# A two-layer decoder trunk on one core: the expert weights of one token block written by accumulating transfers

## The chip, the core and the metric

The kernel runs on one core of a Trainium2 chip. The metric is the device time of one execution in microseconds, the median of several runs. Five engines work beside each other and meet at semaphores: TensorE (PE in the profile) multiplies matrices, VectorE (DVE) and ScalarE (ACT) work element by element, GpSimd (POOL) mostly issues DMAs here, the row fetches among them, and SyncE (SP) issues the loads of the weight panels. Sixteen DMA engines serve all queues together.

## The reference

Two layers, each of a mixer block (three causal token mixers, gated and projected) and an expert block, on 512 tokens of width 1024, all in float32. The change touches the expert block:

```python
def block(xt):                       # 128 tokens at a time
    q = (xt @ w_pq).reshape(PEER_BLOCK, PEER_HEADS, 2, PEER_HALF)
    s = jnp.einsum('thpd,hpkd->thpk', q, sub_keys)
    v1, i1 = lax.top_k(s[:, :, 0], PEER_TOPK)
    v2, i2 = lax.top_k(s[:, :, 1], PEER_TOPK)
...
    top, pos = lax.top_k(cand, PEER_TOPK)
    eidx = jnp.take_along_axis(cidx, pos, axis=-1)
    g = jax.nn.softmax(top.astype(jnp.float32), axis=-1).astype(xt.dtype)
    ue = u_tab[eidx]
    a = jax.nn.gelu(jnp.einsum('thkd,td->thk', ue, xt))
    ve = v_tab[eidx]
    return jnp.einsum('thk,thkd->td', g * a, ve)
```

There are 8 heads, 128 x 128 = 16384 experts a layer, and each token takes 16 experts of each head, 128 in all.

## The kernel before

**Tokens.** The four tiles of 128 tokens are treated in two ways. Tiles 0 to 2, 384 tokens (SD), go densely: every expert's activation is computed for every token, gelu(u_tab @ h), 128 panels of 128 experts a layer, and multiplied by a weight that is zero for nearly all. Tile 3 (DB) goes sparsely: GpSimd fetches the 128 chosen rows of each token from u_tab with indirect DMAs (gather_u, line 700, into six buffers urow), and DVE makes a dot of each (line 1656); later the rows of v_tab follow the same way (gather_v).

**A panel.** A weight panel of 1024 x 128 is loaded by SP into one of four raw buffers, rounded to its high part by ACT (split_hi, line 418), its low part made by DVE (split_lo, line 428), both LEAD = 2 panels ahead, and multiplied by TensorE in 24 matmuls (gemm, lines 441 to 443): 512 columns for the query panels, 384 for the dense experts. ACT takes the output of an expert panel through gelu into hst (post_u, line 1196) and spills it to h_d in device memory. Two PSUM banks alternate.

**Order of a layer's second part.** The heads' stage: for each of 8 heads two query panels and T_U = 8 expert panels, and beside them on DVE the choice of the 16 best (best, rest, pairs, pairs_at, pairs2, places, and key_of in the first two panels of the next head). Behind the last head come the exponential and the division of the softmax for all heads at once, the addresses idu of the row fetches, and 8 more expert panels (M_R1) beside which the first fetches and dots run. Then N_G = 48 groups (M_G): in each an expert panel, and for 8 tokens a one-hot matmul (line 981, each in two passes) that turns the chosen keys and weights of a token into its 128 x 128 weights. DVE builds the one-hot tiles (hot, lines 1665 and 1667), ACT scales one of them (line 1223) and copies the result into stage (line 1247); every fourth group GpSimd writes a block of TB = 32 tokens, 2 MB, to g_d in device memory (line 727). Then 8 more expert panels (M_R2) and the second half: 128 panels of v_tab, for which h_d and g_d are read back (load_h, load_g), multiplied by DVE (weight, line 1698), split and multiplied by TensorE (lines 1001 to 1003), with the sparse tile's v rows beside them (line 1015).

**Queues.** GpSimd's DMAs are one queue in program order, and its waits hold all that follows. It spills and reloads the mixer's gates, loads parameters, fetches rows, writes g_d and reads h_d and g_d. DOTS tells how many dots (and fetches six rows ahead of them) stand beside each panel.

**Start.** norm_h(0, 0) scales the eight chunks of x; DVE makes columns of the modulation in between (first_columns). The first two panels are multiplied pairwise (gemm_two, lines 457 to 459), chunk by chunk as they come, but only when both low splits are there; these stand in the chunk iterations 7 and 8.

## Time and profile before

| | before |
|---|---|
| median of 3 runs | 3568.3 us (3566.43 to 3577.35) |
| the profiled execution | 3572.08 us, its span 3570.3 us |
| TensorE busy | 97% of the span |
| VectorE, ScalarE, GpSimd busy | 69%, 41%, 25% |
| mean granted TensorE clock | 0.986 |
| DMA | 909.83 MB, mean 255 GB/s |

In the profile a row of the time order gives start and duration in us, then engine, line, operation, out<-in and count, and in brackets the idle time of the engine before it with what ended it. Matmuls overlap, so the time that one costs is read from start to start. Numbers of a stretch are busy times of each engine in it. Times count from the span's start.

### The profile page before, as it was taken

The page shows a single profiled execution, that of the slowest core. Times are in us where ns is not written, and L with a number is a line of the kernel's source. Part 1 is how long each engine was busy: PE and PEld are TensorE (multiplying, and loading weights), DVE is VectorE, ACT ScalarE, POOL GpSimd, SP SyncE. Part 2 cuts the span into 40 slices and gives each one's busy share as a digit, 9 for nine tenths or more (in the row PEclk, how much of TensorE's full clock was granted, in tenths as well). Part 3 has the DMA queues.
Part 4 walks back from the last instruction along what each step waited for, and adds up shares of the span by engine and source line. Part 5 has one row for each costly group of instructions (what it writes and reads, how often), then busy time and mean ns, then how long its engine had stood idle before and what let it go on. Part 6 is the DMA issues. An engine that isn't in the chain of part 4 may idle for free.

```text
span 3570.3 us, 54219 instructions
## 1 busy us (share of the span) xinstructions
PE 3475.4 (97%) x18428; PEld 2973.7 (83%) x18428; DVE 2467.0 (69%) x4643; ACT 1462.7 (41%) x2544; POOL 895.4 (25%) x1026
## 2 busy tenths in 40 slices
PE   6999999999999999999999999999999999999998
PEld 5776889999999787777777777999999998777776
DVE  6455678889888775555464556888898878555554
ACT  3324233335877333333233333333367753333332
POOL 0010100003333534444400010000053345344442
PEclk9999999999999999999999999999999999999999
DMA  6354434447999998999744433444499999799995
GB/s 244 126 185 135 142 132 147 149 149 282 354 338 346 391 343 336 363 358 359 292 151 155 161 130 123 149 154 147 147 349 345 344 361 388 278 366 356 364 356 199
DMA packets 269536, 909.83 MB, mean 255 GB/s; under 512 B 32213, under 2 KB 65029, under 8 KB 268453
## 3 DMA queue, kind: packets, MB, share of 16 engines
q0 software_dynamic: 126352, 471.34, 35.9%
q1 hardware_dynamic: 106128, 385.92, 30.8%
q10 hardware_dynamic: 36868, 50.35, 3.8%
q8 instruction: 84, 1.38, 0.2%
q14 instruction: 104, 0.84, 0.1%
HBM read 792.14 MB, written 115.34 MB: 254 GB/s over the span
## 4 chain that ended last, share of the span: by engine, by line
PE 92%; DMA 3%; DVE 2%; issue 1%; POOL 1%; ACT 1%; SPq 0%; DVEq 0%; ACTq 0%; POOLq 0%
PE ps L441 15%; PE ps L443 15%; PE ps L442 15%; PE ps L1001 10%; PE ps L1003 9%; PE ps L1002 9%; PE ps L981 5%; PE ps L1015 3%; PE ps L810 2%; DMA urow<-in_u_rows,idu 1%; PE ps L866 1%; PE ps L937 1%; PE ps L485 1%; DMA hin<-expert_spill 1%; PE ps L887 1%
## 5 line engine op out<-in xcount | busy, mean ns | idle before, releaser
L441 PE MATMUL ps<-mov,whl 128*128 128x384 f32 (+1 forms) x2816 | 1008.8, 358 | 2.2 <-DVE whl L428 2.2
L443 PE MATMUL ps<-mov,whl 128*128 128x384 f32 (+1 forms) x2816 | 985.5, 350 | 0.0
L442 PE MATMUL ps<-mov,whl 128*128 128x384 f32 (+1 forms) x2816 | 984.2, 350 | 0.0
L428 DVE TENSOR_TENSOR whl<-raw,whl 128x1024 fp32r<-128x1024 f32 x648 | 792.5, 1223 | 206.8 <-ACT whl L418 202.5
L418 ACT CAST whl<-raw 128x1024 fp32r<-128x1024 f32 x648 | 679.5, 1049 | 87.4 <-ACT hst L1196 78.8
L1001 PE MATMUL ps<-whl,wgthl 128*128 128x512 f32 x1536 | 608.4, 396 | 19.6 <-DVE wgthl L1710 19.6
L700 POOL DMA_INDIRECT urow<-in_u_rows,idu x256 | 310.8, 1214 | 1208.8 <-DVE idu L1643 778.1
L1003 PE MATMUL ps<-whl,wgthl 128*128 128x512 f32 x1536 | 604.6, 394 | 0.0
L1002 PE MATMUL ps<-whl,wgthl 128*128 128x512 f32 x1536 | 603.4, 393 | 0.0
L441 PEld LDWEIGHTS ps<-mov,whl 128*128 128x128 f32 x2816 | 529.3, 188 | 40.1 <-issue 8.7
L442 PEld LDWEIGHTS ps<-mov,whl 128*128 128x128 f32 x2816 | 529.5, 188 | 30.5 <-issue 2.4
L443 PEld LDWEIGHTS ps<-mov,whl 128*128 128x128 f32 x2816 | 528.5, 188 | 31.6
L1256 ACT CAST wgthl<-wgt 128x384 fp32r<-128x384 f32 x256 | 131.4, 513 | 813.9 <-PE ps L1003 743.8
L1710 DVE TENSOR_TENSOR wgthl<-wgt,wgthl 128x384 fp32r<-128x384 f32 x256 | 142.7, 558 | 358.1 <-ACT wgthl L1256 356.8
L1001 PEld LDWEIGHTS ps<-whl,wgthl 128*128 128x128 f32 x1536 | 290.2, 189 | 108.1 <-issue 25.2
L1003 PEld LDWEIGHTS ps<-whl,wgthl 128*128 128x128 f32 x1536 | 290.1, 189 | 64.3
L1002 PEld LDWEIGHTS ps<-whl,wgthl 128*128 128x128 f32 x1536 | 290.3, 189 | 63.2
L708 POOL DMA_INDIRECT vrow<-in_v_tab,idv x256 | 272.6, 1065 | 252.2 <-PE ps L1015 183.4
L1656 DVE CUSTOM_DVE_ANT_0 urow<-urow,htok 128x1024 f32<-128x1024 f32 x256 | 306.3, 1218 | 34.4 <-DMA urow<-in_u_rows,idu 34.1
L1196 ACT ACTIVATE hst<-ps 128x384 f32<-128x384 f32 x256 | 123.9, 484 | 364.3 <-PE ps L443 344.0
L1223 ACT ACTIVATE hotg<-hotg,gT 128x128 f32<-128x128 f32 x768 | 235.1, 391 | 11.2 <-DVE hotg L1665 11.2
L690 POOL DMA_DIRECT2D hin<-expert_spill x256 | 145.0, 571 | 336.2 <-DVE wgt L1698 315.6
(261 smaller groups left out, 3623.0 us busy)
## 6 DMA issues: line engine op xcount, KB each, us to landing
raw<-in_uT_tab SPq DMA_DIRECT2D x256, 512.0 KB, 4.5
raw<-in_v_tab SPq DMA_DIRECT2D x256, 512.0 KB, 6.9
expert_spill<-hst ACTq DMA_DIRECT2D x256, 192.0 KB
hin<-expert_spill POOLq DMA_DIRECT2D x256, 192.0 KB, 7.9
gt<-weight_spill POOLq DMA_DIRECT2D x64, 768.0 KB, 8.8
weight_spill<-stage POOLq DMA_DIRECT2D x22, 2048.0 KB, 14.7
raw<-in_w_in SPq DMA_DIRECT2D x72, 512.0 KB, 4.7
raw<-in_w_mod SPq DMA_DIRECT2D x64, 512.0 KB, 3.6
```

The lines of the kernel that those rows point to most:

```text
L418: nc.scalar.copy(whl[:, m % RING, 0], raw[:, raw_n(m) % RAW]).then_inc(hi_done, 1)
L428: nc.vector.tensor_tensor(whl[:, m % RING, 1], raw[:, raw_n(m) % RAW], whl[:, m % RING, 0].bitcast(F32), ALU.subtract).then_inc(lo_done, 1)
L441: nc.tensor.matmul(o, w[:, 0, k], src[:, 0, k, :cols], start=(k == 0), stop=False)
L442: nc.tensor.matmul(o, w[:, 0, k], src[:, 1, k, :cols], start=False, stop=False)
L443: mm = nc.tensor.matmul(o, w[:, 1, k], src[:, 0, k, :cols], start=False, stop=(k == KC - 1))
L700: pool.indirect_dma_start(urow[:, k % UR], None, u_rows, bass.IndirectOffsetOnAxis(idu[:, k:k + 1], 0)).then_inc(u_in[k % UR], 16)
L708: pool.indirect_dma_start(vrow[:, slot], None, v_tab.rearrange("a p d -> (a p) d"), bass.IndirectOffsetOnAxis(idv[:, q, j:j + 1], 0)).then ...
L1001: nc.tensor.matmul(o, ghi, hi, start=first, stop=False)
L1002: nc.tensor.matmul(o, ghi, lo, start=False, stop=False)
L1003: mm = nc.tensor.matmul(o, glo, hi, start=False, stop=last)
L1223: ins = nc.scalar.activation(one, one, ACT.Copy, scale=gT[:, e * GT + t:e * GT + t + 1])
L1656: nc.vector.tensor_tensor_reduce(urow[:, k % UR], urow[:, k % UR], htok[:], 1.0, 0.0, ALU.mult, ALU.add, act_in[:, k:k + 1]).then_inc(dot_ ...
```

## The change

One of the three dense tiles, tokens 256 to 383 (N_TS = 1, OHB = 2), gets its weights in another way. Its four blocks of g_d are filled with zeros at the start of each layer's mixer, four DMAs of 2 MB in GpSimd's queue from a zero tile. In the heads' stage DVE computes, one head later, the place in g_d of each of the tile's 16 choices (chosen, seven small operations), and GpSimd adds the weight there with one indirect accumulating DMA for each choice, 128 elements of 4 bytes, one for each token: 16 a head, 128 a layer. For that the softmax is made head by head: the subtraction in places, the exponential on ACT at panel 9, the division on DVE at panel 10 (shares). Before a head's transfers GpSimd waits until the previous head's have landed; the last head's are put one by one among the row fetches behind the stage, and the reading of g_d waits for all.

The groups fall from 48 to 32 a layer, T_U grows from 8 to 10, so the number of panels stays. Of the sparse tile's 128 dots, 28 a layer go into the heads' stage, four for each head from the second on, at panels 9, 10, 11 and 11, with their fetches; DOTS_V is 21 instead of 24. The transposes that feed the fetches' dots (htok) move to the start of the heads' stage, and eight instead of eleven transposes turn the choices. At the very start the high splits of the first two panels stand in chunk iterations 1 and 3, the low ones in 3 and 5.

```diff
-T_U = 8
+T_U = 10
...
-LATE_U = 2 * REST + NTB * BLK_U
-DOTS_V = 24
+LATE_U = 2 * REST + N_G
+DOTS_H = (0, 0, 0, 0, 0, 0, 0, 0, 0, 1, 1, 2)
+DOTS_A = sum(DOTS_H) * (PH - 1)
+DOTS_V = 21
...
+            for b in range(N_OH, NTB):
+                pool.dma_start(g_d[:, :, b].rearrange("a p x -> p a x"),
+                               zero[:].unsqueeze(1).to_broadcast([P, P // AG, P])).then_inc(zero_out, 16)
...
+            def scatter_one(h, n):
+
+                k, t = h * TOPK + n // N_TS, n % N_TS
+                settle(pool)
+                pool.indirect_dma_start(g_d.rearrange("a p b (x o) -> (a p b x) o", o=1),
+                                        bass.IndirectOffsetOnAxis(idg[:, t, k:k + 1], 0),
+                                        topv[:, OHB + t].rearrange("p h k -> p (h k)")[:, k:k + 1], None,
+                                        compute_op=ALU.add).then_inc(sc_out, 16)
+
+            def scatter(h):
+
+                pool.wait_ge(idg_ready, l * PH + h + 1)
+                pool.wait_ge(g_norm, l * PH + h + 1)
+                pool.wait_ge(sc_out, l * (16 * N_TS * SLOTS) + 16 * N_TS * TOPK * h)
+                for n in range(N_TS * TOPK if h + 1 < PH else 0):
+                    scatter_one(h, n)
+
+            pool.wait_ge(zero_out, (l + 1) * (16 * (NTB - N_OH)))
+            for h in range(PH):
+                pool.wait_ge(idu_ready, l * PH + h + 1)
+                if h == 0:
+                    for k in range(UR):
+                        gather_u(k)
+                scatter(h)
+                if h + 1 < PH:
+                    for k in range(h * sum(DOTS_H), (h + 1) * sum(DOTS_H)):
+                        gather_u(k + UR)
+            left = list(range(N_TS * TOPK))
             for n in range(LATE_U):
-                for k in range(dots_by(n - 1) if n else 0, dots_by(n)):
+                for k in range(dots_by(n - 1) if n else DOTS_A, dots_by(n)):
                     if k + UR < SLOTS:
                         gather_u(k + UR)
+                    if left:
+                        scatter_one(PH - 1, left.pop(0))
...
-                if not (l or which) and c >= KC - 3 and c < KC - 1:
-                    split_hi(act, l, c - (KC - 3))
+                if not (l or which) and c in (1, 3):
+                    split_hi(act, l, c // 2)
...
+                    if j == 9:
+                        act.wait_ge(g_sub, l * PH + h + 1)
+                        nc.scalar.activation(topv[:, :, h], topv[:, :, h], ACT.Exp).then_inc(g_exp, 1)
...
-                if not (l or which) and c >= KC - 1:
-                    split_lo(dve, l, c - (KC - 1))
+                if not (l or which) and c in (3, 5):
+                    split_lo(dve, l, c // 2 - 1)
...
+            def chosen(h):
+
+                hs = slice(h * TOPK, (h + 1) * TOPK)
+                first, second = sel1[:, OHB:DB, h], sel2[:, OHB:DB, h]
+                nc.vector.scalar_tensor_tensor(idf[:, 0, hs], sel1[:, DB, h], float(NKEYS), sel2[:, DB, h], ALU.mult, ALU.add)
+                nc.vector.scalar_tensor_tensor(place[:, 1], second, float(NTB * AG), first, ALU.mult, ALU.add)
+                chain.link(nc.vector.tensor_scalar(place[:, 0], first, -1.5, 0.25, ALU.add, ALU.mult))
+                nc.vector.tensor_scalar(idu[:, hs], idf[:, 0, hs], lbase[:], None, ALU.add).then_inc(idu_ready, 1)
+                chain.link(nc.vector.tensor_scalar(place[:, 0], place[:, 0], MAGIC, MAGIC, ALU.add, ALU.subtract))
...
             for h in range(PH):
                 for j in range(2 + T_U):
                     split_lo(dve, l, M_T + h * (2 + T_U) + j + LEAD)
                     if j < 2 and h:
                         key_of(h - 1, j)
+                    if j == 1 and h:
+                        chosen(h - 1)
+                    if j == 10:
+                        shares(h)
+                    if h:
+                        at = (h - 1) * sum(DOTS_H)
+                        dots_between(at + sum(DOTS_H[:j]), at + sum(DOTS_H[:j + 1]))
```

## Rows read from the trace of the kernel before

**Rows 1.** The page: busy us, share, instructions; the chain by engine.

```profile
PE 3475.4 (97%) x18428; PEld 2973.7 (83%) x18428; DVE 2467.0 (69%) x4643; ACT 1462.7 (41%) x2544; POOL 895.4 (25%) x1026
...
PE 92%; DMA 3%; DVE 2%; issue 1%; POOL 1%; ACT 1%; SPq 0%; DVEq 0%; ACTq 0%; POOLq 0%
```

**Rows 2.** Stretches of layer 0: busy us, granted clock, DMA share, GB/s.

```profile
462.00:828.00 366.00, 366.00 (x2046) 351.06 (x2044) 310.87 (x954) 126.32 (x164) 0.00 (x0) 1.00 0.45 148
...
862.00:1146.00 284.00, 283.70 (x1903) 283.41 (x1902) 252.09 (x295) 224.20 (x527) 105.52 (x85) 1.00 0.98 346
```

**Rows 3.** TensorE in time order, two groups of one-hot matmuls.

```profile
903.31 1.95 PE L981 MATMUL ps<-hotg,hot 128*128 128x128 f32 x16
905.01 0.42 PE L441 MATMUL ps<-mov,whl 128*128 128x384 f32 x1
...
909.26 0.94 PE L981 MATMUL ps<-hotg,hot 128*128 128x128 f32 x7
```

**Rows 4.** ScalarE in time order, heads' stage: two panels' output copies.

```profile
533.97 0.49 ACT L1196 ACTIVATE hst<-ps 128x384 f32<-128x384 f32 x1 [2.11 <-PE ps L443]
...
538.13 0.49 ACT L1196 ACTIVATE hst<-ps 128x384 f32<-128x384 f32 x1 [2.11 <-PE ps L443]
```

**Rows 5.** All engines in time order, the end of the first normalization.

```profile
36.71 0.72 ACT L1084 ACTIVATE mov<-ht,mod_cols 128x512 fp32r<-128x512 f32 x1 [3.49 <-DVE ht L1346]
...
43.48 0.75 DVE L1351 SCALAR_TENSOR_TENSOR mov<-ht,mod_cols,mov 128x512 fp32r<-128x512 f32 x1
...
48.83 1.22 DVE L428 TENSOR_TENSOR whl<-raw,whl 128x1024 fp32r<-128x1024 f32 x1
...
50.20 0.79 PE L457 MATMUL ps<-mov,whl 128*128 128x512 f32 x1 [19.18 <-DVE whl L428]
```

**Rows 6.** Stretches again: start-up, and the mixer's first panels.

```profile
35.00:40.00 5.00, 0.00 (x0) 0.00 (x0) 4.89 (x11) 1.44 (x2) 0.00 (x0) 1.00 0.25 98
65.00:105.00 40.00, 40.00 (x169) 30.70 (x168) 24.97 (x26) 16.10 (x23) 0.00 (x0) 1.00 0.59 202
```

**Rows 7.** Instructions grouped by line: busy us, mean ns, idle before them.

```profile
L700 POOL DMA_INDIRECT urow<-in_u_rows,idu x256 | 310.8, 1214 | 1208.8 <-DVE idu L1643 778.1 <-DVE act_in L1656 393.6 <-issue 36.5
L1656 DVE CUSTOM_DVE_ANT_0 urow<-urow,htok 128x1024 f32<-128x1024 f32 x256 | 306.3, 1218 | 34.4 <-DMA urow<-in_u_rows,idu 34.1
```

**Rows 8.** VectorE in time order, heads' stage and first rest panels.

```profile
520.65 0.89 DVE L1544 MAX8 v<-ps 128x8 f32<-128x128 f32 x4 [2.28 <-PE ps L937]
...
548.50 0.23 DVE L1600 CAST abf<-abu 128x128 f32<-128x128 uint32 x1
...
552.68 1.23 DVE L428 TENSOR_TENSOR whl<-raw,whl 128x1024 fp32r<-128x1024 f32 x1 [2.69 <-ACT whl L418]
...
843.39 1.22 DVE L1656 CUSTOM_DVE_ANT_0 urow<-urow,htok 128x1024 f32<-128x1024 f32 x1 [2.32 <-DMA urow<-in_u_rows,idu]
```

**Rows 9.** ScalarE in time order, behind the last head.

```profile
827.69 1.28 ACT L1214 ACT_TABLE_LOAD   x1 [0.43 <-ACT hst L1196]
```

**Rows 10.** GpSimd in time order, one row fetch.

```profile
841.09 0.94 POOL L700 DMA_INDIRECT urow<-in_u_rows,idu  x1 [0.30 <-issue]
```

**Rows 11.** DMA: queues (packets, MB, share); issues (KB, us to landing).

```profile
q1 hardware_dynamic: 106128, 385.92, 30.8%
q10 hardware_dynamic: 36868, 50.35, 3.8%
...
raw<-in_uT_tab SPq DMA_DIRECT2D x256, 512.0 KB, 4.5
...
weight_spill<-stage POOLq DMA_DIRECT2D x22, 2048.0 KB, 14.7
...
out_x<-x_sb SPq DMA_DIRECT2D x8, 256.0 KB, 2.1
```

**Rows 12.** The chain that ended last (start us, us), change to the second half.

```profile
1167.83 18.77 DMA urow<-in_u_rows,idu
```

**Rows 13.** TensorE in time order, its first matmul of the second half.

```profile
1191.12 0.79 PE L1001 MATMUL ps<-whl,wgthl 128*128 128x512 f32 x1 [7.23 <-DVE wgthl L1710]
```

More of the change, by code:

```diff
@@ L45 @@
 GT = 8
-N_G = SD // GT
+N_TS = 1
+OHB = DB - N_TS
+OH = OHB * P
+N_OH = OH // TB
+N_G = OH // GT
 SLOTS = PH * TOPK
@@ L164, in dots_by @@
 def dots_by(p):
-    return sum(DOTS[:p + 1])
+    return DOTS_A + sum(DOTS[:p + 1])
 assert dots_by(LATE_U + DOTS_V - 1) == SLOTS
@@ L919, in _, with turn_rows @@
             spread_root(pe, 2, l * 4 + 4, l * 2 + 2)
+            def turn_rows():
+                for c in range(KC):
+                    o = ps[:, 4 + c // 4, c % 4 * P:(c % 4 + 1) * P]
+                    nc.tensor.matmul(o, mov[:, 0, c, SD:], identr[:], start=True, stop=False)
+                    mm = nc.tensor.matmul(o, mov[:, 1, c, SD:], identr[:], start=False, stop=True)
+                mm.then_inc(htok_turned, 1)
             def two_heads(two, first=False):
@@ L952, in experts @@
                         gemm(pe, l, first_m + j, more=i * 4, more_half=i * 2, cols=SD)
-            for c in range(KC):
-                o = ps[:, 4 + c // 4, c % 4 * P:(c % 4 + 1) * P]
-                nc.tensor.matmul(o, mov[:, 0, c, SD:], identr[:], start=True, stop=False)
-                mm = nc.tensor.matmul(o, mov[:, 1, c, SD:], identr[:], start=False, stop=True)
-            mm.then_inc(htok_turned, 1)
             for n in range(REST):
@@ new lines, in chosen @@
+            def chosen(h):
[6 more added lines that the diff above has]
+                chain.link(nc.vector.tensor_scalar(place[:, 0], place[:, 0], MAGIC, MAGIC, ALU.add, ALU.subtract))
+                chain.link(nc.vector.scalar_tensor_tensor(place[:, 2], place[:, 0], float(P * NTB * AG - AG), place[:, 1],
+                                                          ALU.mult, ALU.add))
+                if l == 0 and h == 0:
+                    dve.wait_ge(tokat_made, P // TB)
+                for t in range(N_TS):
+                    last = nc.vector.tensor_scalar(idg[:, t, hs], place[:, 2, t], float(TB), tokat[:, t:t + 1],
+                                                   ALU.mult, ALU.add)
+                last.then_inc(idg_ready, 1)
```

107 lines of the change are left out of this document (61 added, 46 removed).

## The prediction

> **What bounds the kernel now.** I read the busy times first, then the chain that ended last. TensorE is busy 97% of the span and is 92% of the chain [rows 1], so time comes out where its work comes out, if nothing else turns up late in its place. Next come the stretches of layer 0 [rows 2]: the heads' stage (462 to 828 us), the groups of one-hot matmuls (862 to 1146). In both TensorE never stops, and the DMA share is 0.45 and 0.98. So the heads' stage has room on the DMA engines and the one-hot groups have none. Whether the latter go at TensorE's pace or at the transfers' is the first question.
>
> Start to start answers it. A group starts at 903.31 and the next at 909.26, 5.95 us; the panel inside starts at 905.01, so the 16 passes of one-hot matmuls take 1.70 us and the panel with its restart 4.25 [rows 3]. In the heads' stage the output copies that follow a panel lie 4.16 us apart [rows 4]. A group is thus one panel at TensorE's own pace plus 1.79 us of one-hot work, and at 5.95 us the 284 us of the stretch [rows 2] hold 47.7 of them, which leaves no room for a stop. The transfers just keep up.
>
> **The change part by part.** *One-hot work removed.* The number of groups falls from 48 to 32 a layer, 32 fewer in all. The panels in them are not removed: a head gets ten instead of eight, at 4.16 us. The saving is 32 x (5.95 - 4.16) = 57.3 us [rows 3, 4]. DVE loses two one-hot builds and ScalarE eight scalings and a stage copy for each of these groups; both sit beside TensorE and give nothing. Three transposes of eleven go as well, near 0.11 us each, 0.6 us in both layers, from the start-to-start of such small passes inside [rows 3] (1.70 / 16 = 0.106).
>
> *If the transfers set the pace.* Then bytes must be counted. Sixteen groups of a layer take away 16 x (0.52 + 0.20) MB of panel and spill, four weight writes of 2.1 MB, and 28 row fetches of 0.52 MB move to the heads' stage: 34.5 MB. At the 346 GB/s of that stretch [rows 2] this is 100 us, against 16 x 5.95 = 95 us that the stretch gets shorter. What stays is therefore no denser than before, and both readings give the same saving.
>
> *Start-up.* Today the first paired matmul starts at 50.20, after the second low split of 48.83, which stands behind the last scaled chunk [rows 5]. The low splits now come behind chunk iterations 3 and 5. DVE does the same work in another order: the first split comes ahead of the last columns, and the second ends about 43.48 + 0.67 + 1.2 (the first split) + 1.2 (itself), at 46.6. The engines move 98 GB/s between 35 and 40 [rows 6], so the loads asked for at the start are in by then, and ScalarE's first high split finds its data in the idle 3.49 us before 36.71 [rows 5] or little later. Gain 50.2 - 46.6 = 3.6 us. Five of the eight chunks lie ready by then, and the other three come 1.4 us apart, faster than TensorE takes them. Ends: 0 if the raw panel lands late, 5 if the splits hide in ScalarE's gaps.
>
> *DVE in the heads' stage.* It is busy 310.9 of the 366 us of eight heads, 38.9 of 46 for one [rows 2]. A head now lasts 46.0 + 2 x 4.16 = 54.3 us. Added: two low splits (2.4), four dots of 1.3 (5.2) [rows 7], and some eleven small operations on 16 to 64 columns, 0.23 us for one of 128 columns [rows 8], 2.2 us at 0.2 each. Sum 48.7 of 54.3. Locally it fits as well: the addresses are made where DVE later waits 2.28 us for the key scores, the dots where it waits 2.69 us for ScalarE's split, and two extra panels bring 8.3 us of room there [rows 8]. A low split is still ready one to two panels ahead. Cost 0; without this cover each microsecond of lateness beyond about 2 is TensorE's, 7 heads and 2 layers.
>
> *ScalarE.* One exponential a head instead of one a layer costs two table loads of 1.28 us [rows 9] and 0.3. It comes while the panel before its output copy still runs, and ScalarE waits 2.11 us per panel [rows 4]; the output copy comes about 0.6 us late once a head, and its bank isn't needed for a panel. Cost 0.
>
> *GpSimd.* A row fetch is 1.21 us of issue [rows 7], and 0.30 lies between two [rows 10]. If an accumulating transfer of 128 elements costs the same, 16 of them and 4 fetches take 30 us of a head's 54.3; GpSimd has nothing to do there today (0 busy in 462 to 828 [rows 2]). The wait for the previous head's transfers holds only its own queue, in which the fetches of a head later stand: six fetched rows lie ahead, and a row is wanted about a head after its issue. The last head's 16 go among the fetches of the first rest panels. There two dots per 4.16 us would want 2 x 3 us of GpSimd, but the first six rows have landed already, where today DVE waits 2.32 us for the first [rows 8]. I see the last of these rows 0 to 3 us late and TensorE not held. Cost 0, ends -1 and +6.
>
> *The accumulating transfers in the DMA engines.* No row shows one. Lower end: two queues' shares over their packets [rows 11]. For queue 10 that is 0.038 x 16 x 3570 / 36868 = 59 ns for 1.4 KB, for queue 1 0.308 x 16 x 3570 / 106128 = 166 ns for 3.6 KB; the two lie on a line through zero, so a plain small packet costs next to nothing. Upper end: the quickest landing of any transfer, 2.1 us [rows 11], paid for each of 8 elements per engine one after another. I take a value near the lower end, below 0.15 us an element: a 512 KB panel brings 8 packets to an engine and lands in 4.5 us, not in 8 x 2.1, so packets of a queue overlap. Then a head's transfers are 16 x 8 x 0.15 = 19 us of each engine's 54, with 0.45 taken by panels and spills and 4 fetches of 1.3 us: 24 + 19 + 5 = 48 of 54. Cost 0.
>
> The Trainium skill, page "DMA: Bandwidth & Descriptors", section Specifications, says that below 512 B a transfer doesn't reach line rate because the engine reads, modifies and writes; it speaks against a 4-byte scatter, and no row here shows what one costs. By its fixed cost of about 2.0 us for each DMA issued from GpSimd, 16 in a row would be an estimated 32 us of a head, which fits too, and the sum would stay.
>
> *Zero fill.* Four writes of 2 MB a layer at the mixer's start, behind the two projection weights in GpSimd's queue. A 2 MB write lands in 14.7 us even at a DMA share of 0.98 [rows 11]. Between 65 and 105 us the engines move 202 GB/s [rows 6], against 346 where they are full [rows 2], so 8.4 MB find room in some 50 us. What it may hold is the panel and modulation loads, which have about two panels of lead. Cost 0, ends 0 and 10 us in both layers.
>
> *The change to the second half.* TensorE stops 7.23 us there [rows 13], behind a row fetch that took 18.77 us [rows 12] because weights, spills and rows are all read at once. The same transfers in the same order stay. It neither grows nor goes; +-5 us for both layers.
>
> **Sum.** 57.3 + 0.6 + 3.6 = 61.5 us off the profiled execution's 3572.1: 3510.6. Its time is 3.8 us above the median of the three runs and inside their range, so for the median 3568.3 - 61.3 = 3507.0.
>
> **Rivals.** *Scatter-bound, slower.* Accumulates that go one after another fill the heads' stage. With 24 us of panels and spills and 5 of fetches in 54.3, they decide from 25 / 128 = 0.2 us an element. At 0.3 us a head needs 24 + 5 + 38 = 67 us, 13 more, in 14 heads 182; rows fetched a head ahead lend up to 54 us a layer, which leaves 74: 3507 + 74 = 3581, and far more at 0.5. For it: read and write-back of the same bytes is more than any packet of before does. Against it: packets overlap. *Partly eaten.* The engines pass from queue to queue, and a burst of small elements delays the spill writes (two buffers, 8.3 us) or the panels: 2 us for one panel in each of 14 heads, 28 us, and 10 us of zero fill give 3507 + 38 = 3545. The Trainium skill, page "DMA: Bandwidth & Descriptors", section Queues, rings and completion order, says that an engine turns between queues only at the end of a packet, so that eight elements of a scatter, if they make one packet, would hold it in one piece; no row here shows that. *Nothing gained.* The one-hot groups are held by something that the heads' stage meets too, DVE's total above all: 3568. It would need 61 us of lateness where DVE has 5.6 us to spare in each head; unlikely.
>
> **Chances and range.** Forecast case (3495 to 3522) 0.66; partly eaten (3522 to 3557) 0.14; nothing gained 0.05; scatter-bound 0.15. The range 3494 to 3555 holds the first two. About 0.3% (11 us) is what a measurement can tell from no change. Faster 0.80, same 0.05, slower 0.15.
>
> **What would show it.** The heads 54.3 us apart with panels of 4.16, and no idle time of TensorE between them; 32 groups a layer at 5.95; the first paired matmul at 46.6; the scatters 1.5 us apart on GpSimd and the last of a head landed before the next head's begin; the stop at the second half between 5 and 10 us. Wrong would be: DVE waiting for rows inside a head, ScalarE waiting for its spill writes, GpSimd standing at the wait for a head's transfers into the next head.

## The result and the profile after

The changed kernel took 3553.8 us (median of 8 runs, 3550.2 to 3560.6); the kernel before, run beside it, took 3574.0 (8 runs, 3566.4 to 3577.4). The ratio is 0.9948, with a 95% interval of 0.9937 to 0.9958: 20 us faster, 0.5%. The forecast was 61 us. The direction was right, the size was a third of it, and 41 us have to be accounted for: 42 by the two profiled executions, which the rows below go by.

The profiled execution took 3553.5 us and its span is 3551.3, against 3570.3 before. First the page of the kernel after: span and instructions, busy us of each engine with its share, the chain by engine, and queue 0 of the DMA (packets, MB, share of 16 engines).

```profile
span 3551.3 us, 53170 instructions
...
PE 3441.6 (97%) x17910; PEld 2919.2 (82%) x17910; DVE 2420.1 (68%) x4725; ACT 1401.7 (39%) x2298; POOL 1368.3 (39%) x1287
...
q0 software_dynamic: 163216, 471.49, 38.7%
...
PE 86%; DMA 4%; DVE 4%; POOL 2%; issue 2%; ACT 1%; SPq 0%; ACTq 0%; DVEq 0%; POOLq 0%
```

Two things differ from [rows 1]. GpSimd is busy 39% of the span where it was 25%. And TensorE is 86% of the chain where it was 92%: DMA, DVE, GpSimd and bare issue time have come in. Its busy time fell by 33.8 us only, so not all of the 57 us of removed one-hot work shows even there: other work of TensorE's has become slower.

Where the time went is read by stretches. I cut both traces at the same instructions of TensorE and took the time from one cut to the next (us):

| stretch, from its first TensorE work to the next one's | before, layer 0 / 1 | after, layer 0 / 1 | forecast of the difference | measured, both layers |
|---|---|---|---|---|
| start-up, to the first paired matmul | 50.2 | 46.6 | -3.6 | -3.6 |
| first projections of layer 0, with what precedes them | 51.3 | 53.2 | 0 | +1.9 |
| change between layers, start of layer 1 | 19.5 + 52.0 | 20.8 + 60.0 | 0 | +9.3 |
| rest of the mixers | 354.4 / 356.8 | 354.6 / 355.1 | 0 | -1.5 |
| heads' stage | 397.5 / 396.7 | 463.8 / 464.2 | +133.1 | +133.8 |
| selections turned, to the first group | 13.7 / 13.7 | 13.4 / 13.4 | -0.6 | -0.6 |
| groups and rest panels, to the second half | 324.1 / 324.7 | 239.6 / 240.1 | -190.4 | -169.1 |
| second half | 592.4 / 598.6 | 601.2 / 600.6 | 0 | +10.8 |
| end | 24.6 | 24.9 | 0 | +0.3 |

The heads' stage and the start-up came out as the steps said. Three lines did not: the groups lack 21.3 us of their saving, the two starts cost 11 less the 1.5 of the rest, about 10, and the second half, which the prediction left alone but for its first stop, is 10.8 longer. That is the 42 us. In the other profiled kernels with the same heads' stage it is 134.8 to 138.4 us longer than before, not 133.8; the kernel after had the shortest of them.

**The groups.** Windows of the kernel after (from:to, length, busy us of PE, PEld, DVE, ACT and POOL with their instructions, granted clock, DMA share, GB/s): the heads' stage, layer 0's groups, their first part, and a piece of that.

```profile
462.00:912.00 450.00, 450.00 (x2532) 435.45 (x2531) 390.36 (x1118) 180.44 (x228) 245.76 (x148) 1.00 0.67 193
...
931.00:1171.00 240.00, 224.23 (x1453) 222.67 (x1451) 190.78 (x228) 160.25 (x360) 123.86 (x93) 0.98 0.97 340
...
932.00:990.00 58.00, 54.89 (x368) 54.28 (x367) 47.41 (x55) 40.92 (x97) 49.47 (x31) 1.00 0.89 262
...
989.00:1000.00 11.00, 6.35 (x43) 6.03 (x42) 5.28 (x6) 4.78 (x11) 3.25 (x3) 0.88 0.97 355
```

In the heads' stage TensorE is busy 450.0 of 450.0 us, with the DMA share risen from 0.45 [rows 2] to 0.67. In the second window it is busy 224 of 240 us. Some 7.4 us of the difference are the stop at the second half, which the window reaches and which was there before; the rest are stops in the groups, where the kernel before had none. GpSimd is busy 49.5 of the first 58 us. Between 989 and 1000 TensorE works little more than half of the time and its granted clock is 0.88 on average, that is, behind the stop part of the stretch went at the lower of its two levels.

TensorE of the kernel after in time order (start, us, line and operation, idle time before it and what ended it):

```profile
931.66 1.95 PE L1040 MATMUL ps<-hotg,hot 128*128 128x128 f32 x16
...
940.67 2.02 PE L1040 MATMUL ps<-hotg,hot 128*128 128x128 f32 x16 [2.88 <-issue]
...
946.70 1.95 PE L1040 MATMUL ps<-hotg,hot 128*128 128x128 f32 x16
...
989.02 1.95 PE L1040 MATMUL ps<-hotg,hot 128*128 128x128 f32 x16
...
999.81 3.77 PE L1040 MATMUL ps<-hotg,hot 128*128 128x128 f32 x16 [4.65 <-ACT hotg L1283]
```

From 946.70 to 989.02 there are seven steps of 6.05 us, and in the quiet part before 989.02 they are 5.97, close to the 5.95 of [rows 3]. But the second group starts 9.0 us behind the first, and the one at 999.81 comes 10.8 behind the one at 989.02; its sixteen passes take 3.77 us instead of 1.95, which is the slower clock, and the step to the next group takes 8.2. These three steps of 9.0, 10.8 and 8.2 carry 10.1 of the 10.7 us that layer 0 loses against 31 steps of 5.97; layer 1 loses 10.8, at its first, second, tenth and eleventh step. Who was late is on VectorE and GpSimd of the same kernel:

```profile
935.72 1.23 DVE L1705 CUSTOM_DVE_ANT_0 urow<-urow,htok 128x1024 f32<-128x1024 f32 x1 [2.38 <-DMA urow<-in_u_rows,idu]
...
994.73 1.22 DVE L1705 CUSTOM_DVE_ANT_0 urow<-urow,htok 128x1024 f32<-128x1024 f32 x1 [7.58 <-DMA urow<-in_u_rows,idu]
```

```profile
908.82 1.07 POOL L726 DMA_INDIRECT urow<-in_u_rows,idu  x1 [12.02 <-DVE act_in L1705]
...
910.19 2.63 POOL L741 DMA_INDIRECT weight_spill<-topv,idg  x1 [0.30 <-issue]
913.13 1.34 POOL L726 DMA_INDIRECT urow<-in_u_rows,idu  x1 [0.30 <-issue]
914.78 2.59 POOL L741 DMA_INDIRECT weight_spill<-topv,idg  x1 [0.30 <-issue]
917.67 1.95 POOL L726 DMA_INDIRECT urow<-in_u_rows,idu  x1 [0.31 <-issue]
...
971.47 2.60 POOL L741 DMA_INDIRECT weight_spill<-topv,idg  x1 [0.30 <-issue]
974.37 1.36 POOL L726 DMA_INDIRECT urow<-in_u_rows,idu  x1 [0.30 <-issue]
...
977.66 1.79 POOL L780 DMA_DIRECT2D weight_spill<-stage  x1
```

VectorE waits for a fetched row, 2.4 and then 7.6 us, and builds the next group's one-hot tiles late. The row is late because GpSimd issues without a gap: every row fetch now carries one accumulating transfer of the last head behind it. From the fetch at 908.82 to the one at 974.37, 16 such pairs, it is 65.55 us: **4.10 us a pair**, where the rest panels want two rows in 4.16 us and the groups three in 11.9. GpSimd stays behind until the 16 are gone, and the first weight write of the groups, due with the fourth group, is queued behind them too and goes out at 977.66. What follows at once is a burst of held-back fetches together with 2 MB of weights; a fetch in it takes 14.95 us to land (chain of the kernel after, start and us):

```profile
979.75 14.95 DMA urow<-in_u_rows,idu
```

**The starts.** ScalarE and TensorE of the kernel after, the start of layer 1:

```profile
1817.76 1.04 ACT L433 CAST whl<-raw 128x1024 fp32r<-128x1024 f32 x1 [11.59 <-DMA raw<-in_w_in]
...
1819.35 2.07 PE L493 MATMUL ps<-sq,ones 128*128 128x512 f32 x2 [7.02 <-ACT sq L489]
```

ScalarE stands 11.6 us before the split of a panel that has not come, and TensorE stops 7.0 us behind it. Here the zero fill is under way; GpSimd of layer 0, and then the DMA issues (KB each, median us to landing), show it:

```profile
56.81 5.09 POOL L677 DMA_DIRECT2D weight_spill<-zero  x3 [0.30 <-POOL zero L674]
...
97.01 1.69 POOL L677 DMA_DIRECT2D weight_spill<-zero  x1 [35.10 <-issue]
```

```profile
weight_spill<-zero POOLq DMA_DIRECT2D x8, 2048.0 KB, 23.1
```

Three writes go out at once, the fourth stands 35 us in its queue, and they land after 23 us in the median, the slowest after 36. A panel load asked for meanwhile lands in 9.7 to 13.5 us, where the median of all of them is 5.0 (chain of the kernel after, three panel loads):

```profile
63.09 11.31 DMA raw<-in_w_in
86.47 9.66 DMA raw<-in_w_in
...
1804.28 13.45 DMA raw<-in_w_in
```

**The second half.** No stop has come there. TensorE's first matmul of it, in the kernel after, waits 7.36 us, against 7.23 [rows 13]:

```profile
1171.23 0.79 PE L1060 MATMUL ps<-whl,wgthl 128*128 128x512 f32 x1 [7.36 <-DVE wgthl L1797]
```

Instead nearly every step is longer. ScalarE's split of the second-half weights comes once a panel of 18 matmuls, and its start-to-start is the step; first the kernel before, then the kernel after:

```profile
1221.82 0.51 ACT L1256 CAST wgthl<-wgt 128x384 fp32r<-128x384 f32 x1 [2.65 <-PE ps L1003]
...
1225.93 0.52 ACT L1256 CAST wgthl<-wgt 128x384 fp32r<-128x384 f32 x1 [2.65 <-PE ps L1003]
```

```profile
1606.40 0.51 ACT L1316 CAST wgthl<-wgt 128x384 fp32r<-128x384 f32 x1 [2.73 <-PE ps L1062]
...
1610.60 0.51 ACT L1316 CAST wgthl<-wgt 128x384 fp32r<-128x384 f32 x1 [2.73 <-PE ps L1062]
```

4.11 against 4.20 us, and ScalarE waits for TensorE both times, so TensorE itself is slower. By the matmuls' starts, 181 of the 256 steps of the kernel before take 4.12 us, and some 186 of the kernel after 4.20; the others are longer in both. Over 256 panels 0.08 us is 20 us at most. The matmuls and their operands are the same, and in plain stretches of 80 us around these rows TensorE is busy throughout at a granted clock of 1.00 in both. What differs is where the tiles lie: the changed program declares new small tiles and shorter ones, and `wgthl`, the stationary operand of these matmuls, has moved by 800 bytes, from address 181056 to 180256 in each partition (worked out, as every address below, from the sizes of the tiles that the kernel declares ahead of it). `whl`, the moving operand, is declared ahead of everything that changes and has not moved in any kernel here.

### The profile page after: what moved, and what is told of

It reads as the page before. It is cut to its first block, busy times and chain, and to the rows that moved or that the text cites. A ratio compares the mean times of both kernels' runs of the same rounds, so it can differ in the third digit from the quotient of the medians.

```text
span 3551.3 us, 53170 instructions
## 1 busy us (share of the span) xinstructions
PE 3441.6 (97%) x17910; PEld 2919.2 (82%) x17910; DVE 2420.1 (68%) x4725; ACT 1401.7 (39%) x2298; POOL 1368.3 (39%) x1287
## 3 DMA queue, kind: packets, MB, share of 16 engines
q0 software_dynamic: 163216, 471.49, 38.7%
## 4 chain that ended last, share of the span: by engine, by line
PE 86%; DMA 4%; DVE 4%; POOL 2%; issue 2%; ACT 1%; SPq 0%; ACTq 0%; DVEq 0%; POOLq 0%
PE ps L456 14%; PE ps L458 13%; PE ps L457 13%; PE ps L1060 10%; PE ps L1062 10%; PE ps L1061 10%; PE ps L1074 3%; DMA urow<-in_u_rows,idu 2%; PE ps L1040 2%; PE ps L864 2%; POOL weight_spill L741 1%; DMA raw<-in_w_in 1%; PE ps L920 1%; DVE urow L1705 1%; PE ps L1000 1%
## 5 line engine op out<-in xcount | busy, mean ns | idle before, releaser
L741 POOL DMA_INDIRECT weight_spill<-topv,idg x256 | 470.6, 1838 | 185.7 <-DVE idg L1696 111.3
L726 POOL DMA_INDIRECT urow<-in_u_rows,idu x256 | 323.1, 1262 | 507.7 <-DVE act_in L1705 300.7
L734 POOL DMA_INDIRECT vrow<-in_v_tab,idv x256 | 264.8, 1035 | 258.9 <-PE ps L1074 190.0
```

What stands on the lines that cost most here:

```text
L726: pool.indirect_dma_start(urow[:, k % UR], None, u_rows, bass.IndirectOffsetOnAxis(idu[:, k:k + 1], 0)).then_inc(u_in[k % UR], 16)
L734: pool.indirect_dma_start(vrow[:, slot], None, v_tab.rearrange("a p d -> (a p) d"), bass.IndirectOffsetOnAxis(idv[:, q, j:j + 1], 0)).then ...
L741: pool.indirect_dma_start(g_d.rearrange("a p b (x o) -> (a p b x) o", o=1), bass.IndirectOffsetOnAxis(idg[:, t, k:k + 1], 0), topv[:, OHB ...
```

## The experiments

Three theories were to be told apart: the groups by GpSimd's issue time or by the accumulates' elements in the DMA engines; the starts by the zero fill; the second half by addresses or by the transfers beside it. "Groups" below is the time from the first group to the second half, layer 0 / layer 1 (after: 239.6 / 240.1); "second half" likewise (before 592.4 / 598.6, after 601.2 / 600.6), and "steps" are its usual panel steps. Every ratio is to the kernel before, run beside the kernel in question; the diffs show the lines that matter and leave out those that follow from them.

### One cause at a time

**The new tile at the other end.** All other tiles move down by 32 bytes, `wgthl` to 180224.

```diff
-    tokat = sb("tokat", [P, N_TS])
+    tokat = sb("tokat", [P, N_TS], at=(nc.sbuf_usable_end - 64) // 32 * 32)
```

> The changed kernel with its new 32-byte tile tokat at the end of the memory, so that every tile behind it lies 32 bytes lower and starts at a multiple of 64 again; the instructions are the same. In the changed kernel a panel of the second half takes 4.20 us where the kernel before takes 4.12, in both layers. Theory A (the start of wgthl at an odd multiple of 32 bytes costs the step): panels of 4.12 us, 256 x 0.08 = 20 us less than the changed kernel's 3554, near 3534. Rival B (the step comes from the order of the instructions or from chance): 4.20 us and 3554 as before.

3549.3 us, ratio to before 0.9932 [0.9915, 0.9948]. The steps of the second half are 4.17 to 4.20 us. It came out as no theory had it: 180224 is a multiple of 64, as 181056 is, and its steps are still not 4.12. The 4.5 us that the median fell are not in the second half; they lie in the groups, 237.3 / 235.1, which vary that much from one kernel to another.

**The last head's accumulates later, behind every second row.**

```diff
-                    if left:
+                    if left and n >= REST and k % 2 == 0:
```

> The changed kernel with the last head's 16 accumulating transfers behind every second row fetch from the first one-hot group on, not behind each fetch of the first rest panels. Theory A (GpSimd's issue time, 1.84 + 0.3 us for an accumulate and 1.3 + 0.3 for a fetch, makes the rows late and the first weight write with them): the stops of 3.2 and 4.8 us in the one-hot groups go, the stretch from the first group to the second half falls from 239.6 to about 229 us in each layer, 17 to 21 us less in all, near 3535. Rival B (the small elements in the DMA engines are what delays the rows): the stops move or stay, 3550 to 3556.

3534.9 us, ratio 0.9888 [0.9871, 0.9904]. Groups 230.0 / 229.4, where the forecast for the changed kernel was 229. Same accumulates, same elements, same bytes, another place in GpSimd's queue. The window is that of the first part of the groups, columns as above:

```profile
932.00:990.00 58.00, 58.00 (x392) 58.00 (x392) 53.85 (x65) 45.70 (x109) 45.66 (x26) 1.00 0.98 331
```

TensorE does not stop at all in it (54.9 of 58 in the kernel after) and the transfers go at 331 GB/s instead of 262.

**The zero writes one by one**, each behind a gate spill of the projections, instead of four in a row at the mixer's start.

```diff
-            for b in range(N_OH, NTB):
-                pool.dma_start(g_d[:, :, b].rearrange("a p x -> p a x"),
-                               zero[:].unsqueeze(1).to_broadcast([P, P // AG, P])).then_inc(zero_out, 16)
...
+                if j % 4 == 3 and j < 16:
+                    pool.dma_start(g_d[:, :, N_OH + j // 4].rearrange("a p x -> p a x"),
+                                   zero[:].unsqueeze(1).to_broadcast([P, P // AG, P])).then_inc(zero_out, 16)
```

> The changed kernel with the four zero writes of a layer behind the gate spills 3, 7, 11 and 15 and not one after another at the mixer's start. Theory A (the zero fill delays the panel loads, which land in 9 to 15 us in place of 4): the stop of 7.4 us in layer 1 and that of 1.6 us in layer 0 go, 8 to 10 us less, near 3545. Rival B (the stop is due to something else that is early in the mixer, the place is free elsewhere too): no change, 3554; a gate spill that waits behind 2 MB would even cost some us.

3546.7 us, ratio 0.9921 [0.9904, 0.9937]. First projections 51.1 and 51.8 us, where the kernel after has 53.2 and 60.0 and the kernel before 51.3 and 52.0. The zero fill was the cause of the slow starts, and it was its timing: the same bytes cost nothing when they come apart, and land in 13.3 us instead of 23.1.

**The kernel before with its tiles moved by 32 bytes.**

```diff
     eps = sb("eps", [P, 1])
+    pad = sb("pad", [P, 1])
```

> The kernel before with 32 bytes of padding behind eps and nothing else, so that every tile behind it starts at an odd multiple of 32 bytes, as in the changed kernel. Theory A (address): panels of the second half take 4.20 us, 15 to 20 us more than before, 3589 to 3594. Rival B (not the address): 4.12 us and the time of before.

3585.9 us, ratio 1.0033 [1.0021, 1.0046]: 11.5 us slower by a tile that nobody uses. Steps 4.20 us, second half 601.2 / 603.0, as in the kernel after. The size is below what was expected, since the step was forecast for all 256 and the kernel before has 75 that were longer than 4.12 to begin with.

**The changed kernel with every old tile at its old address**; its new tiles lie at the end and the shortened ones keep their full size.

```diff
-    tokat = sb("tokat", [P, N_TS])
+    tokat = sb("tokat", [P, N_TS], at=nc.sbuf_usable_end // 32 * 32 - 32)
...
-    gT = sb("gT", [P, OH])
-    place = sb("place", [P, 3, N_TS, TOPK])
-    idg = sb("idg", [P, N_TS, SLOTS], U32)
+    gT = sb("gT", [P, SD])
+    place = sb("place", [P, 3, N_TS, TOPK], at=nc.sbuf_usable_end // 32 * 32 - 224)
+    idg = sb("idg", [P, N_TS, SLOTS], U32, at=nc.sbuf_usable_end // 32 * 32 - 736)
```

> The changed kernel with every tile of the kernel before back at its address of before (the new small tiles at the end of the memory, sel1T, sel2T and gT at their old sizes); the work is the same. The padding of 32 bytes alone had put the kernel before to 4.20 us a panel. Theory A (the step is a matter of the addresses): 4.12 us for the panels of the second half in both layers, 18 to 20 us less than the changed kernel, 3532 to 3537. Rival B (the changed kernel's other instructions hold it at 4.20 too): 3549 to 3554.

3541.1 us, ratio 0.9903 [0.9886, 0.992]. Steps 4.12 us, second half 592.7 / 591.1, 18.0 us less than in the kernel after. So with all transfers of the change in place the second half is that of before: addresses, not transfers. The groups, 241.8 / 238.1, stay as long as they were.

### Which tile it is

**The padding between `wgt` and `wgthl`** of the kernel before, so that only `wgthl` and two tiles behind it move.

```diff
     wgt = sb("wgt", [P, 2, SD])
+    pad = sb("pad", [P, 1])
     wgthl = sb("wgthl", [P, 2, 2, SD], F32R)
```

> The kernel before with 32 bytes between wgt and wgthl, so that only wgthl, otok and e32 move; all else stays. Theory A (the place of wgthl, TensorE's stationary tile of the second half, sets the step): panels of 4.17 to 4.20 us, 3584 to 3590. Rival B (it is hst, hin, wgt, the stage or another tile of those that the padding moved): 4.12 us, 3574.

3587.6 us, ratio 1.004 [1.0024, 1.0056], steps 4.20 us, second half 602.0 / 605.8. `wgthl` it is, or one of the two behind it, which these matmuls do not read.

**64 bytes instead of 32**, once with all tiles moved and once with `wgthl` and the two behind it alone.

```diff
-    pad = sb("pad", [P, 1])
+    pad = sb("pad", [P, 16])
```

> The kernel before with 64 bytes of padding behind eps. Theory A (only an odd multiple of 32 bytes costs): 4.12 us a panel, 3574. Rival B (it is the distance between addresses or their place within a larger unit; the kernel with everything 32 bytes lower had 4.17 to 4.20 at an even multiple): anything from 4.12 to 4.20, up to 3590.

> The kernel before with 64 bytes between wgt and wgthl, so that only wgthl, otok and e32 move. Theory A (the address of wgthl alone sets the step, as 32 bytes at the same place did with 4.20): 4.08 us a panel of the second half, 256 x 0.04 = 10 us less, 3560 to 3564. Rival B (the gain of the padding behind eps needs the others' new places too): 4.12 us, 3573.

3558.7 us, ratio 0.9958 [0.9942, 0.9974], and 3564.1 us, ratio 0.9974 [0.9958, 0.999]. Both have steps of 4.08 us, and second halves of 589.8 / 591.8 and 591.7 / 591.6: the kernel before becomes 0.3 to 0.4% faster by an unused tile of 64 bytes. ScalarE's splits, with the 32 bytes and then with the 64, `wgthl` moved in both:

```profile
1603.05 0.51 ACT L1257 CAST wgthl<-wgt 128x384 fp32r<-128x384 f32 x1 [2.74 <-PE ps L1004]
...
1607.25 0.51 ACT L1257 CAST wgthl<-wgt 128x384 fp32r<-128x384 f32 x1 [2.73 <-PE ps L1004]
```

```profile
1600.88 0.51 ACT L1257 CAST wgthl<-wgt 128x384 fp32r<-128x384 f32 x1 [2.61 <-PE ps L1004]
...
1604.95 0.51 ACT L1257 CAST wgthl<-wgt 128x384 fp32r<-128x384 f32 x1 [2.61 <-PE ps L1004]
```

### Issue time or elements

The changed kernel, with the last head's accumulates replaced by fillers: after each of the 16 fetches GpSimd clears a small tile that nobody reads, 6, 8 or 10 times. That takes GpSimd's time and moves nothing; the last head's weights of this tile are left out of the output, and two waits count 16 landings fewer.

```diff
                     if left:
-                        scatter_one(PH - 1, left.pop(0))
+                        left.pop(0)
+                        for _ in range(BUSY):
+                            busy_steps.link(nc.gpsimd.memset(busy[:], 0.0))
```

Six:

> The changed kernel in which the last head's 16 accumulating transfers of a layer are left out (their weights are missing in the output) and GpSimd instead fills a small unused tile six times in a row, some 2 us, at each of their places: the issue time stays, the small elements in the DMA engines are gone. Theory A (issue time on GpSimd is what makes the rows late): the stretch from the first group to the second half stays at 236 to 242 us in each layer, near 3554. Rival B (the elements in the DMA engines): 229 us, near 3534.

3539.5 us, ratio 0.9903 [0.9883, 0.9922], groups 229.5 / 229.5. By the number this is the theory of the elements. But GpSimd's rows show that the filler was too short:

```profile
912.13 1.07 POOL L730 DMA_INDIRECT urow<-in_u_rows,idu  x1 [12.01 <-DVE act_in L1711]
...
968.73 1.31 POOL L730 DMA_INDIRECT urow<-in_u_rows,idu  x1 [0.80 <-POOL busy L776]
```

16 pairs in 56.60 us, 3.54 a pair against 4.10. So this kernel alone cannot tell the theories apart. Eight and ten:

> As the run with six fills, but eight: with six a fetch and its fills took 3.60 us together, where a fetch and an accumulate take 4.09 in the changed kernel (61.28 us for 15 pairs), and the stops were gone. Eight fills bring the pair to 4.03 us, with none of the small elements (the last head's weights are missing in the output again). Theory A (issue time, with a threshold between 3.6 and 4.1 us a pair): the stops are back, 234 to 242 us from the first group to the second half. Rival B (the elements in the DMA engines, or the time that the engine's ring is full): 229.5 us again.

> Ten fills, 4.46 us a pair, the last head's weights missing again. Theory A: stops longer than in the changed kernel, 240 to 250 us. Rival B: 229.5 to 232 us.

Eight: 3553.2 us, ratio 0.9946 [0.9924, 0.9969]; ten: 3565.9 us, ratio 0.9979 [0.9968, 0.999]. Their rows, the first fetch of the 16 pairs and the one behind the last pair, eight and then ten:

```profile
911.45 1.07 POOL L730 DMA_INDIRECT urow<-in_u_rows,idu  x1 [12.01 <-DVE act_in L1711]
...
973.71 1.86 POOL L730 DMA_INDIRECT urow<-in_u_rows,idu  x1 [0.80 <-POOL busy L776]
```

```profile
912.97 1.07 POOL L730 DMA_INDIRECT urow<-in_u_rows,idu  x1 [12.01 <-DVE act_in L1711]
...
981.47 1.54 POOL L730 DMA_INDIRECT urow<-in_u_rows,idu  x1 [0.80 <-POOL busy L776]
```

| kernel | pair on GpSimd, us | groups, layer 0 / 1 | lost against 31 steps of 5.97 |
|---|---|---|---|
| fillers, 6 | 3.54 | 229.5 / 229.5 | 0.1 / 0.2 |
| fillers, 8 | 62.26 / 16 = 3.89 | 237.2 / 234.7 | 7.5 / 5.7 |
| after, accumulates | 65.55 / 16 = 4.10 | 239.6 / 240.1 | 10.7 / 10.8 |
| fillers, 10 | 16 pairs in 68.50 = 4.28 | 241.7 / 245.5 | 12.6 / 16.7 |

The kernel after lies between the fillers of eight and ten, as its pair does. Without one element of the last head moved, the groups get longer from a pair somewhere between 3.5 and 3.9 us on, and they lose it at the same steps: with eight fillers the first takes 6.4 us, the tenth 9.5 and the eleventh 8.9. Nor do the fills slow VectorE beside them: it is busy 2420.3 us in all with ten, 2420.1 in the kernel after. Layer 0's groups with eight fillers (columns as in the windows above; the window ends in the stop at the second half):

```profile
932.00:1169.00 237.00, 226.87 (x1463) 225.00 (x1461) 188.78 (x225) 159.76 (x359) 113.38 (x166) 0.98 0.96 343
```

So GpSimd's issue time alone makes a loss of this size. That the elements add some microseconds on top can't be excluded: with the accumulates in place, the four kernels whose groups are the same (after, the new tile moved, the zero writes apart, the old addresses) lose 6.6 to 12.4 us a layer, and up to 5 us lie between two layers of one kernel.

### The split move alone

The kernel before, with nothing but the splits of the first two panels moved: the high ones behind the second and fourth chunk, the low ones behind the fourth and sixth.

```diff
-                if not (l or which) and c >= KC - 3 and c < KC - 1:
-                    split_hi(act, l, c - (KC - 3))
+                if not (l or which) and c in (1, 3):
+                    split_hi(act, l, c // 2)
...
-                if not (l or which) and c >= KC - 1:
-                    split_lo(dve, l, c - (KC - 1))
+                if not (l or which) and c in (3, 5):
+                    split_lo(dve, l, c // 2 - 1)
```

> The kernel before with only the first two panels' splits moved to chunk iterations 1, 3 (high) and 3, 5 (low). Theory A: the first paired matmul at 46.6 instead of 50.2 us and the mixer's rest unchanged, 3.6 us less. Rival B (the next panels' loads or splits set the pace and take it back): the pair early, the projections at 101.5 as before, no gain.

3569.6 us (10 runs, 3565.7 to 3575.0), ratio 0.9993 [0.9983, 1.0002]. The time alone can't tell 3.6 us, a thousandth. The profile can: TensorE's first paired matmul of this kernel is at 47.12, not 50.20 [rows 5].

```profile
47.12 0.79 PE L457 MATMUL ps<-mov,whl 128*128 128x512 f32 x1 [15.63 <-DVE whl L428]
```

It has the first projections behind it at 98.0 us instead of 101.5 and reaches the first group at 863.3 instead of 867.0. The three microseconds are kept.

### All three causes taken away

**Together**: old addresses, accumulates behind every second row of the groups, zero writes apart.

> Three repairs at once in the changed kernel: addresses of before, the last head's accumulates behind every second fetch from the first one-hot group on, the zero writes behind the gate spills. If the three causes are separate, the gains add: 3554 - 19 - 19 - 7 = 3509, 65 us less than the kernel before. Rival (they share one cause, or the next stop takes over): 3520 to 3535.

3505.4 us, ratio 0.9813 [0.9797, 0.983]. Groups 228.7 / 228.2, second half 592.8 / 592.1, first projections 51.7 / 50.8: each stretch at the forecast or at its length before the change. It is 68.7 us less than the kernel before beside it (61 to 73 by the interval), where 61 were forecast for the changed kernel, so the three causes are the whole of what was missed. The single gains, 18.9, 7.1 and 12.7 us against the kernel after, add up to 38.7, and together they bring 48.4. By stretches the singles do add: 20.3 us in the groups, 10.3 in the two first projections and 18.0 in the second half are 48.6, and the joint kernel gains 22.8, 10.7 and 16.9 in the same, 50.4. But in each of the three kernels the heads' stage is 3.0 to 4.5 us longer, both layers together, than in the kernel after, and in the joint one 4.5; the sum of the single gains pays this three times, the joint kernel once. Why it is longer there is not shown.

**With 64 and with 128 bytes of padding on top:**

```diff
     eps = sb("eps", [P, 1])
+    pad = sb("pad", [P, 16])
```

> The kernel with all three repairs, and 64 bytes of padding behind eps, the shift that took 15 us off the kernel before. Theory A (the step of a panel follows the address of wgthl alone, 4.08 us at this one): 256 x 0.04 = 10 us less than 3505, and a few more if the stop at the first v rows goes as well, 3490 to 3497. Rival B (the gain of the padding was in the meeting of transfers and doesn't carry over): 3505.

> The same with 128 bytes of padding, wgthl at 960 in its KB of addresses (832 gave 4.12 us, 896 gave 4.08, 864 and 32 gave 4.20, 0 gave 4.17 to 4.20). This looks for the rule. If even multiples of 32 within the last part of the KB are good: 4.08 and 3495. If it falls off towards the multiple of 1 KB: 4.12 to 4.17, 3505 to 3518.

64 bytes: **3498.2 us** (3497.5 to 3501.2), ratio 0.979 [0.9774, 0.9806], steps 4.08 us, second half 587.9 / 587.3. It is the best kernel here, 75 us faster than before and 56 faster than after. From its page:

```profile
span 3495.4 us, 53170 instructions
...
PE 3403.0 (97%) x17910; PEld 2914.1 (83%) x17910; DVE 2420.3 (69%) x4725; ACT 1401.3 (40%) x2298; POOL 1384.5 (40%) x1287
...
PE 92%; DVE 3%; DMA 2%; issue 1%; POOL 1%; ACT 1%; another core or an unknown queue 0%; SPq 0%; DVEq 0%; ACTq 0%; POOLq 0%
```

As many instructions as the kernel after, GpSimd even a little busier, and TensorE again 92% of the chain. 128 bytes: 3526.0 us, ratio 0.9865 [0.9845, 0.9885], steps 4.20, second half 601.8 / 602.4. The expectation had the quick steps here, or near them; it was wrong, and with it both rules that it offered for the addresses.

## Why the prediction was right and wrong

**Right: what a group costs.** The heads' stage grew by 133.8 us for 32 panels, 4.18 each where 4.16 was taken from [rows 4] (4.2 to 4.3 in the other kernels of the changed program), and the groups got as short as 228 to 230 us in every kernel in which nothing else was late, which is the forecast's 324 - 95. The reading of [rows 3], one panel at TensorE's own pace plus 1.79 us of one-hot work, carried the whole sum.

**Right: start-up and cover.** The first paired matmul is at 46.6, as worked out. In the heads' stage VectorE is busy 390 of 450 us and TensorE 450 of 450: no cost on VectorE or ScalarE, as said. The stop at the second half is 7.4 us, inside 5 to 10.

**Right: the elements.** The rival "scatter-bound", and what "partly eaten" put on them, fell. Queue 0 carries 163,216 packets, and in the kernel before:

```profile
q0 software_dynamic: 126352, 471.34, 35.9%
```

36,864 packets more (256 x 128 = 32,768 of them the elements) with the same bytes, and 2.8 points more of share: 0.028 x 16 x 3551 / 36,864 = 43 ns a packet, were all of it theirs. That is below the 0.15 us taken, and far from the 0.2 us at which the heads' stage would have been bound. The 16 of a head are issued within 33 us.

**Wrong: GpSimd, the term "cost 0, ends -1 and +6".** The step that failed is its premise: an accumulate was taken to cost what a fetch costs, 1.21 + 0.30. Grouped by line, the kernel after has (busy us, mean ns, idle before):

```profile
L741 POOL DMA_INDIRECT weight_spill<-topv,idg x256 | 470.6, 1838 | 185.7 <-DVE idg L1696 111.3 <-issue 74.4
L726 POOL DMA_INDIRECT urow<-in_u_rows,idu x256 | 323.1, 1262 | 507.7 <-DVE act_in L1705 300.7
```

1.84 + 0.30 us for 512 bytes of elements, half as much again as for 512 KB of rows; the 16 of layer 0's rest panels and groups took 2.15 in the mean, 1.6 to 2.6. "The scatters 1.5 us apart on GpSimd" was the sign that was looked for, and they are 2.1 apart. In the heads' stage it was harmless: 16 are 34 of a head's 54 us. In the rest panels the prediction had "2 x 3 us" of GpSimd for each 4.16 us and saw rows "0 to 3 us late and TensorE not held". Even that pace was slower than the rows were wanted, and its answer was the six rows that lie ahead; but the queue falls back by 2 us a panel, and what stands behind the 16 (the weight write, the fetches of the groups) was not followed. At 2 x 4.1 us it falls back twice as fast, and each layer loses 10.7 us, above the upper end of 6. At the pace that the prediction had, the verdict "TensorE not held" would have been right: with a pair of 3.54 us, longer than its 3.0, nothing was lost. The price of the accumulate is the step that failed. The Trainium skill, page "DMA: Bandwidth & Descriptors", section Anatomy of one DMA, has about 2.0 us of fixed cost for one DMA issued from GpSimd, and says that most of it is the wait until the write is confirmed, not its issue. The prediction had taken it as the spacing of 16 in a row and worked out 32 us by it. The trace has 33 us for them, from 580.98 to 614.2, but that doesn't make the page's figure a rule for the spacing: fetches, which are issued from GpSimd as well, take 1.26 + 0.30 us each. The estimate stood beside the sum where it changed nothing, in the heads' stage, and a price near it was not tried in the one place where it mattered.

**At its end: the zero fill, "cost 0, ends 0 and 10 us in both layers".** It took about 10. What failed was the step from room on average to no delay: with 144 GB/s free, 8.4 MB go in 58 us. The bytes did find their room, but came all at once; a panel load landed in 10 to 13 us instead of 5, and ScalarE and then TensorE stopped for it in spite of the panels' lead of two. What the average hid is shown by the writes that come apart and cost nothing.

**Missing: the second half.** The sum has no term for it but the stop. That a change of tiles elsewhere moves `wgthl` and with it 256 steps by 0.08 us was in none of the steps or rivals, and it made 11 to 13 us of the 42: 10.8 by the second half's lengths, 12.7 by the time of the kernel with the old addresses. Of the second half itself it made 18.0, by the lengths of that kernel; the kernel before had lost 6 us more in layer 1 than in layer 0 (598.6 against 592.4) to something that the kernel after does not show, and whose cause is open. That the range held the time, by one microsecond, was luck. Of its rival "partly eaten" the 10 us of zero fill came true, the 28 us of late spills or panels in the heads did not: TensorE did not stop there.

## What to carry to other kernels

Cost a transfer at the engine that issues it, at its own duration, wherever it stands in a queue that others need; a DMA with almost no bytes may be the dearest to issue, and it belongs where its engine has gaps (here behind every second row of the groups: 19 us for one condition in the code). Ask of a background transfer when it is asked for, not only whether its bytes find room. And when a stretch that nobody touched gets a constant per cent longer, compare the addresses of its operands first: an unused tile of 32 or 64 bytes tells in one run.

## What was not expected of the hardware

**The address of a matmul's stationary tile.** 18 matmuls of 512 columns with `wgthl` as stationary operand took, by the address of `wgthl` in the partition:

| `wgthl` at | remainder by 1024 | step, us | kernels |
|---|---|---|---|
| 180224 | 0 | 4.17 to 4.20 | new tile at the end |
| 180256 | 32 | 4.20 | after |
| 181056 | 832 | 4.12 | before, old addresses |
| 181088 | 864 | 4.20 | two kernels with 32 bytes of padding |
| 181120 | 896 | 4.08 | three kernels with 64 bytes |
| 181184 | 960 | 4.20 | 128 bytes |

From end to end it is 3% of a step and 27 to 28 us of the whole: 3585.9 against 3558.7 with 32 and 64 bytes in the kernel before, 3526.0 against 3498.2 with 128 and 64 in the mended one. The steps are the same for the same address in different programs, and the moves of `wgthl` with two tiles behind it, which these matmuls do not read, show that no other matmul operand is needed for it. Whether it is the weight load or the matmul that is slower, and by which rule, is open.

**Accumulating indirect transfers.** 1.84 us of GpSimd (1.53 to 2.64) for 128 elements of 4 bytes, against 1.26 us for 128 rows of 4 KB; on the DMA engines they cost some 43 ns a packet, by the shares of queue 0. The time is not a constant: in the kernel after 148 of the 256 took less than 1.65 us, and of the 49 that ran beside a dot of VectorE 37 took longer. Whether VectorE's work is the cause was not tried.

**Four writes of 2 MB in a row.** The fourth held GpSimd's queue for 35.1 us in layer 0 and 31.8 in layer 1, with nothing else to wait for in the profile. In layer 0 it went out at 97.0, and the slowest of the three ahead, issued between 56.8 and 61.9, took 36.2 us to land, so it may have waited for them; the profile doesn't name the wait.
